# The two gates of a recurrent unit: two block-diagonal products replaced by four products on quadrants of the array

## The reference

```python
def rglru_branch(xb, conv_w, conv_b, wa, ba, wx, bx, lam):
    xc = causal_dwconv(xb, conv_w) + conv_b
    xh = xc.reshape(Bsz, S, LRU_HEADS, LRU_HEAD_DIM)          # 8 heads x 64
    r = jax.nn.sigmoid(jnp.einsum('bshi,hij->bshj', xh, wa).reshape(Bsz, S, BR) + ba)
    ig = jax.nn.sigmoid(jnp.einsum('bshi,hij->bshj', xh, wx).reshape(Bsz, S, BR) + bx)
    log_a = -LRU_C * r * jax.nn.softplus(-lam)
    a = jnp.exp(log_a)
    mult = jnp.sqrt(-jnp.expm1(2.0 * log_a))
    _, h = lax.associative_scan(linear_combine, (a, mult * ig * xc), axis=1)
```

## Time and profile before

| | us |
|---|---|
| median of 3 runs | 1719.53 |
| lowest, highest | 1717.32, 1721.11 |
| profiled execution, its own time | 1719.88 |
| its span, first to last instruction | 1718.1 |
| granted TensorE clock, mean over the span | 0.982 of 2.4 GHz |

### The profile page before, as it was taken

The page is one execution under the profiler, slowest core; times in us unless marked ns, Lnnn a source line. Parts: engine busy times, 40 slices in busy tenths (PEclk is TensorE's granted clock), DMA queues, the critical chain, the costliest instruction groups (busy, mean ns, idle before and its releaser), DMA issues.

```text
span 1718.1 us, 22890 instructions
## 1 busy us (share of the span) xinstructions
PE 1653.5 (96%) x7696; PEld 1269.4 (74%) x7696; DVE 1164.0 (68%) x2325; ACT 754.4 (44%) x988; POOL 179.4 (10%) x245
## 2 busy tenths in 40 slices
PE   5889999999999999999999999999999999999996
PEld 0347778778777877878887777777877777777885
DVE  1438975995697589657867685588378458743758
ACT  1316535554553555421127454654555465432112
POOL 2001111111111111000001111111111111100000
PEclk9799999999999999999999999999999999999998
DMA  9998899999999998978748888888988888775524
GB/s 364 339 317 212 204 245 245 219 220 221 242 226 231 238 220 204 215 248 274 246 145 203 196 206 195 205 199 208 209 203 208 192 200 204 188 184 218 196 94 116
DMA packets 317297, 373.58 MB, mean 217 GB/s; under 512 B 30584, under 2 KB 227536, under 8 KB 314512
## 3 DMA queue, kind: packets, MB, share of 16 engines
q1 hardware_dynamic: 288608, 270.57, 49.4%
q0 software_dynamic: 27936, 101.72, 33.1%
q10 hardware_dynamic: 656, 0.17, 0.0%
HBM read 263.89 MB, written 10.99 MB: 160 GB/s over the span
## 4 chain that ended last, share of the span: by engine, by line
PE 74%; DVE 17%; DMA 5%; issue 3%; ACT 1%; DVEq 0%; SPq 0%; ACTq 0%
PE bank L1232 19%; PE bank L1187 15%; PE bank L1197 15%; PE bank L1188 14%; DVE work L1562 6%; DMA pro<-in_w_ada 4%; PE bank L1219 2%; DVE work L1421 1%; DVE work L1422 1%; DVE y_t L1570 1%; PE bank L915 1%; DVE carry L1570 1%; DVE ada_acc L1570 1%; PE bank L1127 1%; PE bank L966 1%
## 5 line engine op out<-in xcount | busy, mean ns | idle before, releaser
L1187 PE MATMUL bank<-op,w_hi 128*128 128x512 f32 x1456 | 581.5, 399 | 0.2 <-ACT w_hi L671 0.2
L1188 PE MATMUL bank<-op,w_hi 128*128 128x512 f32 x1456 | 569.1, 391 | 0.0
L671 ACT ACTIVATE w_hi<-raw 128x1024 fp32r<-128x1024 f32 x188 | 199.2, 1059 | 418.9 <-PE bank L1188 286.5
L1197 PE MATMUL bank<-op,w_lo 128*128 128x512 f32 x1456 | 361.9, 391 | 3.6 <-DMA w_lo<-raw 3.6
L1187 PEld LDWEIGHTS bank<-op,w_hi 128*128 128x128 f32 x1456 | 274.1, 188 | 77.7 <-issue 21.6
L1197 PEld LDWEIGHTS bank<-op,w_lo 128*128 128x128 f32 x1456 | 273.7, 188 | 62.7 <-DMA w_lo<-raw 6.0
L1188 PEld LDWEIGHTS bank<-op,w_hi 128*128 128x128 f32 x1456 | 274.3, 188 | 56.6 <-issue 1.9
L604 POOL DMA_DIRECT2D w_lo<-raw x190 | 165.3, 870 | 1333.3 <-ACT w_lo L674 1124.3
L674 ACT ACTIVATE w_lo<-raw 128x1024 fp32r<-128x1024 f32 x188 | 198.4, 1055 | 98.1 <-PE bank L1197 96.6
L1232 PE MATMUL bank<-w_hi,op 128*128 128x512 f32 x960 | 232.2, 392 | 2.1 <-ACT op L861 2.1
L1232 PEld LDWEIGHTS bank<-w_hi,op 128*128 128x128 f32 x960 | 181.0, 189 | 41.0 <-issue 3.2
(11 more groups left out here) (228 smaller groups left out, 1521.1 us busy)
## 6 DMA issues: line engine op xcount, KB each, us to landing
raw<-in_w_in SPq DMA_DIRECT2D x192, 512.0 KB, 4.6
w_lo<-raw POOLq DMA_DIRECT2D x190, 512.0 KB, 5.3
ada_in<-in_w_ada SPq DMA_DIRECT2D x256, 256.0 KB, 4.6
pro<-in_w_ada SPq DMA_DIRECT2D x32, 1024.0 KB, 10.1
raw<-in_w_out SPq DMA_DIRECT2D x64, 512.0 KB, 4.7
y_t<-in_x SPq DMA_DIRECT2D x2, 2048.0 KB, 12.9
bias_t<-bias_rows_scratch SPq DMA_DIRECT2D x16, 256.0 KB, 5.7
y_t<-in_x SPq DMA_DIRECT2D x4, 1024.0 KB, 8.1
```

What stands on the lines that cost most here:

```text
L671: act.activation(w_hi[:, n % NHL, :], raw[:, n % NRAW, :], ACT.Copy).then_inc(s.hi_done.sem, 1)
L1187: pe.matmul(o, w_hi[:, n % NHL, w], op_hi[k], start=k == 0, stop=False)
L1188: mm = pe.matmul(o, w_hi[:, n % NHL, w], op_lo[k], start=False, stop=False)
L1197: mm = pe.matmul(o, w_lo[:, m % NHL, w], op_hi[k], start=False, stop=k == KT - 1)
```

## The change

The weights of a gate are kept as [128, 64], two heads above each other, without zeros. The memset is gone, the four transfers become two. Each gate is two products of 64 rows by 64 columns, and the four products of the two gates are put on four different quadrants of the array: the first gate's heads on the diagonal (rows 0 to 63 to partitions 0 to 63 of bank 5, rows 64 to 127 to partitions 64 to 127), the second gate's heads crosswise, so that they land swapped in bank 6. ScalarE reads bank 6 in two halves of 64 partitions and swaps them back. Both banks' waits are now taken ahead of the first product, with a no-op between.

```diff
-        lru_w = sb("lru_w", [P, 2, P])
+        lru_w = sb("lru_w", [P, 2, 64])
...
-            s.mix_in = signal("mix_in" + n, 96)
+            s.mix_in = signal("mix_in" + n, 64)
...
                     for i, name in enumerate(("lru_wa", "lru_wx")):
                         src = A[name][l].rearrange("h i j -> (h i) j")
-                        for h in range(2):
-                            at = step * P + 64 * h
-                            sp.dma_start(lru_w[64 * h:64 * h + 64, i, 64 * h:64 * h + 64], src[at:at + 64, :])\
-                                .then_inc(s.mix_in.sem, 16)
+                        sp.dma_start(lru_w[:, i, :], src[step * P:(step + 1) * P, :]).then_inc(s.mix_in.sem, 16)
...
-            pool.memset(lru_w[:, :, :], 0.0).then_inc(const_done.sem, 1)
...
                         act.activation(lru_s[0], bank[5][:, :], ACT.Tanh, scale=0.5,
                                        bias=lru_c[:, l, bass.ds(ct + 4, 1)]).then_inc(s.free[5].sem, 1)
-                        act.activation(lru_s[1], bank[6][:, :], ACT.Tanh, scale=0.5,
-                                       bias=lru_c[:, l, bass.ds(ct + 8, 1)]).then_inc(s.free[6].sem, 1)
+                        for h in range(2):
+                            heads, at = slice(64 * h, 64 * h + 64), 64 * (1 - h)
+                            e = act.activation(lru_s[1][heads, :], bank[6][at:at + 64, :], ACT.Tanh, scale=0.5,
+                                               bias=lru_c[heads, l, bass.ds(ct + 8, 1)])
+                        e.then_inc(s.free[6].sem, 1)
...
                         for i in range(2):
                             is_free(5 + i, 0)
-                            fill(5 + i, pe.matmul(bank[5 + i][:, :], lru_w[:, i, :], xc, start=True, stop=True))
+                        pe.nop(nofuse=True)
+                        for i in range(2):
+                            for h in range(2):
+                                heads, to = slice(64 * h, 64 * h + 64), 64 * (h ^ i)
+                                mm = pe.matmul(bank[5 + i][to:to + 64, :], lru_w[heads, i, :], xc[heads, :],
+                                               start=True, stop=True)
+                            fill(5 + i, mm)
```

More of the change, by code:

```diff
@@ L892, in _ @@
             pe.sem_inc(layers[0].hi_used.sem, NHL)
-            pe.wait_ge(const_done.sem, 12)
+            pe.wait_ge(const_done.sem, 11)
             pe.wait_ge(setup_dma.sem, 32)
@@ L1082, in lru_gates @@
                         pe.wait_ge(s.xc_done.sem, s.xc_done.at(1, ct))
-                        pe.wait_ge(s.mix_in.sem, s.mix_in.at(96, ct))
+                        pe.wait_ge(s.mix_in.sem, s.mix_in.at(64, ct))
                         pe.wait_ge(s.p_copy.sem, s.p_copy.at(0, ct))
@@ L1446, in score_max @@
                         if t == 0 and h == 0:
-                            dve.wait_ge(s.mix_in.sem, s.mix_in.at(96, ct))
+                            dve.wait_ge(s.mix_in.sem, s.mix_in.at(64, ct))
                         if t == ST - 1 and h == 1:
@@ L1590, in _ @@
             line(dve.tensor_copy(cond_rep, repeat(cond[:, :], 32)), steps)
-            dve.wait_ge(const_done.sem, 12)
+            dve.wait_ge(const_done.sem, 11)
             own(dve.tensor_copy(j_row[:, :], j_int[:, :]), sched)
```

## The result

The changed kernel takes 1727.96 us (median of 6 runs, 1725.65 to 1728.80); the kernel before, taken beside it, 1718.90 (6 runs, 1717.32 to 1721.11). The ratio is 1.0048, interval 1.0038 to 1.0059. It is slower, by about 9 us, where 1717.7 was forecast and 1723.7 was the upper end. Two executions in a slower state, one of the kernel before (2396.65 us) and one of hi_in_5_pieces (2763.00 us), are in no ratio and in no median given here. Numbers of single steps come from one traced execution of each kernel.

The account below looks back on a forecast made before the run. TensorE (96% busy) bounds, with half-unit 9's w_lo transfer nearly as long a path; 0.26 us gained in each of seven steps, 1.8 off 1719.88, and 0.35 for the median, gave 1717.7 us, range 1715.5 to 1723.7.

Parts of the forecast that it names:

- The gates on TensorE: Last record before the gates to second matmul after: 2.17 us becomes 1.68, 0.49 less, if all four quadrants run together.
- The gates seen by ScalarE: ScalarE starts the gates 0.65 us earlier, the extra half activation costs 0.6; half-unit 9's split moves by -0.05.
- What is late next: TensorE waits for half-unit 9's w_lo transfer; landing 0.1 us shorter; gain 0.26 of 0.49 us per step, seven times 1.8.
- Step 0 of layer 0: The one step unlike the other seven: VectorE hides TensorE's 0.49 us, so no gain, and the extra activation costs nothing.
- The edits without price: Merged lru_w loads, dropped memset, no-op and moved waits: all hidden; the last two 0.1 us per step if not.
- Nothing is left: Extra activation costs 0.69 us, or w_lo's transfer is slowed by 0.1: about 0 per step, 1719.5 to 1720.3 us; 14%.
- The gain is kept whole: Half-unit 9's transfer not in the way: seven times 0.49 = 3.4 us gained, 1716.1 us; 12%.
- The slower rival: Two row halves cannot write one bank at once, so quadrants don't run together: 1723.7 to 1726.5 us; 14%, plus 2%.
- The forecast's own sign of being wrong: TensorE's wait for w_lo at half-unit 9: about 0.2 us expected; absent, 0.4 or more, or staggered gate records refute it.

Follow-up runs that it names:

- hi_in_5_pieces: Kernel before, with the first half of half-unit 9's split copied in five pieces of columns in seven of the eight steps: 1720.81 us, ratio 1.0002.
- after_raw_later: Changed kernel, with SyncE holding half-unit 11's raw load until TensorE finished half-unit 8, except in step 0 of layer 0: 1716.62 us, ratio 0.9977.

## Why the prediction was wrong, step by step

**The gates on TensorE: right.** 1.68 forecast, 1.67 measured, eight times; the four quadrants overlap, and the extremes of a record are 589 and 640 ns. The two banks are each written by two row halves at once. The rule of the Trainium skill, "TensorEngine Tiling (Array Packing)", Gotcha 1: PSUM Pressure, that different row tiles can't access the same bank at the same time, is not borne out here, where the two row tiles write different partitions of the bank: no loss of overlap shows in these records.

**The gates seen by ScalarE: the first mis-sized term.** I charged the extra activation with 0.6, "between 0.58 and the 0.69 that one takes alone", and called it an assumption that the halves are as long as a whole. That part was right (0.69 each). What I missed is that the two neighbours also lose their overlap: 0.98 in all. The trace of before had such activations of 64 partitions in the unit d_u, 0.61 apart at 0.60 long, without overlap; I had not drawn them in. ScalarE's start was as forecast: its table load begins 1.60 us after the last matmul ahead of the gates, against 1.55 to 1.60. But half-unit 9's w_lo is issued 0.36 later than before, counted from that matmul, instead of 0.05 earlier.

**What is late next: the right mechanism, and the term that failed.** TensorE does wait for w_lo, seven times, as forecast, but 2.0 us on average and not 0.2. The step says "I take 0.1 less, between 0.15 less and 0.1 more" for the landing; it measured 1.2 more (7.0 on average against 5.8 before). My one row for a close neighbour was the earlier trace rows, 0.67 behind, with 5.66; from this I took the landing as flat. It is flat from 1.26 down to 0.77 by the runs and 0.67 by that row, and then rises by 1.3 us until 0.3. I overlooked that the trace of before had a closer neighbour, at another w_lo transfer, 0.31 us behind (transfer, raw load, time to landing):

```profile
233.12 0.86 POOL L604 DMA_DIRECT2D w_lo<-raw  x1 [6.68 <-ACT w_lo L674]
...
233.43 0.43 SPq L382 DMA_DIRECT2D raw<-in_w_in  x1
```

```profile
DMA to landing us min/median/max: 7.6/7.6/7.6
```

Other loads stand close to it too, so it would not have given the price, but it spoke against a bound of 0.1 more. ScalarE's 0.4 us too much is what moved the distance from the 0.70 that I expected to 0.28, over that edge. Counted from the last matmul ahead of the gates, the weight load comes 1.7 later than forecast, 0.4 by the issue and 1.3 by the landing; seven times this is 11.9. Layer 0 recovers a part of it. Had the landing stayed flat, the activation's 0.38 too much, seven times, would have brought about 1720.4 (an estimate from these numbers), still inside the range; it is the landing, the term of 0.1 that measured 1.2, that took the time out of it.

**Step 0 of layer 0: wrong in sign.** It gains nothing, as forecast, but "an extra activation costs nothing there" held only for the wait next to it. The period from its gates to the next is 1.5 longer in the changed kernel (150.95 against 149.41; 151.23 in after_raw_later, which leaves this step as in the changed kernel, against 148.98 to 150.37 in the six kernels with the step of before). There w_lo goes out behind its raw load, TensorE's weight loads wait 1.39 for it, and 42 us later its matmuls wait 3.53 (0.37 before).

**The edits without price: not separated, and nothing speaks against.** The no-op and the moved waits leave no hole in front of the gates: their first record starts 0.31 us after the one before, as the row pack of the earlier trace rows does (0.32). The opening up to the first gates is 1.0 us shorter in the changed kernel, but over all runs it scatters between 148.4 and 152.0 us, the kernels with unchanged gates among them, so nothing can be put down to the two merged loads or the memset.

**The rivals.** "Nothing is left" named both causes (an activation of 0.69, a landing 0.1 longer) and priced them at zero net, because it let each stop at the nearest row. "The gain is kept whole" is what came as soon as one of the two was taken away (1714.4 to 1716.6, against 1716.1). The slower rival had the right sign and the wrong mechanism. The forecast's own sign of being wrong, a wait of 0.4 or more, did appear.

## What to carry to other kernels

Where a transfer lands 0.1 us ahead of its use, price what feeds it, not the engine that the edit speeds up: here 0.5 us off TensorE was worth nothing until the transfer's issue was either earlier or alone. An edit that splits one activation into two halves of the partitions pays for the full columns twice and for the overlap with both neighbours; splitting by columns is nearly free. And when two queues' transfers are near each other in time, read their distance in the trace and treat a closer approach than any row shows as unknown to the high side; a constant wait that holds the less urgent one back can do as much as making the urgent one early (1714.5 and 1714.8 here). Look for such pairs in the whole trace, not only at the place of the edit.

## What the runs showed of the hardware

The landing of half-unit 9's accumulating transfer into w_lo depends, not evenly but with an edge, on how far behind it another queue issues a plain load: 5.1 us at a distance of 1.9, 5.7 from 1.26 down to 0.77, mixed at 0.50, 7.0 at 0.30, and the same 7.0 whether ScalarE's halves, ScalarE's pieces or the whole change brought them together. Why the edge lies between 0.77 and 0.30 is not settled by these runs, nor why other transfers into w_lo with the load 2.49 behind took up to 7.9. The Trainium skill, "DMA: Bandwidth & Descriptors", section "Queues, rings and completion order", says that each DMA engine takes turns between the queues that have work, a packet at a time. That the load makes the transfer slower agrees with it; that 0.5 us more or less of head start decides over 1.3 us is not in it, and no run here looks inside a transfer.

Activations of 64 partitions that start at partition 64, or read from there, do not overlap their neighbours: 0.68 to 0.72 from start to start at 0.69 long, against 0.58 for full ones.

Four fp32 products of 64 rows and 64 columns in disjoint quadrants take 1.67 us by the measure of the earlier trace rows, although two of them write the same bank from different rows, to different partitions.

After a gap of 3.53 us in the matmuls the granted clock was 0.56 from 209.80 to 213.20 us, near the lower of its two levels (1.2 of 2.4 GHz); after the gaps of 1.43 to 1.74 us at half-unit 9 in the seven steps it was 1.00.
